# Swapping the halves of queries and keys: transfers within the on-chip memory in place of products with signed permutations

## The reference, cut to what matters

```python
def apply_rope(x, cos, sin):
    half = x.shape[-1] // 2
    x1, x2 = x[..., :half], x[..., half:]
    return jnp.concatenate([x1 * cos - x2 * sin, x1 * sin + x2 * cos], axis=-1)

qa = axial_rope(rms_norm(qa, q_norm_a), cos_r, sin_r, cos_c, sin_c)   # A: 8 heads of 64, rotated in two groups of 32
ka = axial_rope(rms_norm(ka, k_norm_a), cos_r, sin_r, cos_c, sin_c)   # A: 2 key heads
q_rope = apply_rope(q_rope, cos_t, sin_t)                             # B: 8 heads, 32 features of each
k_rope = apply_rope(kr, cos_t, sin_t)                                 # B: one key part of 32 features
```

## Time and profile before

| | us |
|---|---|
| median of three runs | 2465.02 (2460.68 to 2466.03) |
| span of the profiled execution | 2457.9 |
| PE busy | 2368.7 (96%) |
| DVE busy | 1412.9 (57%) |
| ACT busy | 1138.7 (46%) |
| POOL busy | 894.2 (36%) |

### The profile page before, as it was taken

How to read it: one execution, slowest core, us unless ns; L and a number is a source line. 1 busy time by engine, 2 the same in 40 slices (tenths; PEclk the granted TensorE clock), 3 DMA queues, 4 the chain that set the end, 5 groups by cost and what they waited for, 6 DMA issues and landing times.

```text
span 2457.9 us, 31373 instructions
## 1 busy us (share of the span) xinstructions
PE 2368.7 (96%) x12074; PEld 1954.5 (80%) x12074; DVE 1412.9 (57%) x1963; ACT 1138.7 (46%) x1778; POOL 894.2 (36%) x665
## 2 busy tenths in 40 slices
PE   5999999989999999999999999999999999999998
PEld 5778788868888888876678877788878888888887
DVE  6255499958885330139963753332576666666665
ACT  5322388868884221249952474231333333333334
POOL 1111234236652112335521222112255555555651
PEclk8999999999999999999999999999999999999999
DMA  7244300000003131100031311013111111111121
GB/s 301 75 129 145 94 6 1 1 19 1 1 1 112 59 108 43 52 1 1 10 112 38 121 44 43 18 35 120 43 52 52 52 52 52 52 52 52 52 60 69
DMA packets 152487, 143.21 MB, mean 58 GB/s; under 512 B 10358, under 2 KB 140692, under 8 KB 150420
## 3 DMA queue, kind: packets, MB, share of 16 engines
q1 hardware_dynamic: 152340, 141.22, 18.0%
HBM read 124.43 MB, written 16.78 MB: 57 GB/s over the span
## 4 chain that ended last, share of the span: by engine, by line
PE 81%; ACT 8%; issue 5%; DVE 4%; POOL 1%; DMA 1%; SPq 0%; ACTq 0%; DVEq 0%; POOLq 0%
PE ps L260 38%; PE ps L2608 14%; PE ps L2625 9%; PE ps L1103 4%; PE ps L1126 3%; PE ps L1113 3%; ACT C_PR L1773 1%; ACT B_PR L1186 1%; ACT B_PTH L1180 1%; PE ps L2584 1%; PE ps L1662 1%; ACT C_PTH L1781 1%; PE ps L2052 1%; PE ps L2064 1%; PE ps L1641 1%
## 5 line engine op out<-in xcount | busy, mean ns | idle before, releaser
L249 POOL TENSOR_TENSOR WL<-WR,WH 128x1024 fp32r<-128x1024 f32 (+1 forms) x89 | 207.5, 2332 | 827.3 <-ACT WH L244 827.2
L260 PE MATMUL ps<-HH,WH 128*128 128x512 f32 (+1 forms) x1136 | 362.3, 400 | 0.0
L260 PE MATMUL ps<-HL,WH 128*128 128x512 f32 (+1 forms) x1136 | 353.4, 392 | 0.0
L260 PE MATMUL ps<-HH,WL 128*128 128x512 f32 (+1 forms) x1136 | 352.7, 392 | 0.0
L260 PEld LDWEIGHTS ps<-HL,WH 128*128 128x128 f32 (+1 forms) x1136 | 213.9, 188 | 47.3
L260 PEld LDWEIGHTS ps<-HH,WL 128*128 128x128 f32 (+1 forms) x1136 | 213.9, 188 | 47.1
L260 PEld LDWEIGHTS ps<-HH,WH 128*128 128x128 f32 (+1 forms) x1136 | 210.0, 189 | 51.8 <-issue 10.1
L2838 DVE TENSOR_TENSOR XF<-ps,XF 128x1024 f32<-128x1024 f32 x168 | 201.5, 1220 | 32.4 <-PE ps L2625 25.8
L2608 PE MATMUL ps<-HC,WSH 128*128 128x512 f32 x640 | 197.0, 389 | 0.0
L1139 DVE TENSOR_REDUCE NM<-ps 128x1 f32<-128x1024 f32 x128 | 156.0, 1220 | 35.0 <-PE ps L1103 34.1
L2525 POOL TENSOR_TENSOR WSL<-WSR,WSH 128x512 fp32r<-128x512 f32 x100 | 131.0, 1310 | 107.6 <-ACT WSH L2519 107.6
(11 more groups left out here) (433 smaller groups left out, 5227.2 us busy)
## 6 DMA issues: line engine op xcount, KB each, us to landing
WS<-in_w_ffn_in SPq DMA_DIRECT2D x44, 512.0 KB, 5.0
MKW<-in_ada_w SPq DMA_DIRECT2D x32, 512.0 KB, 4.1
spill<-X SPq DMA_DIRECT2D x3, 4096.0 KB, 13.6
OW<-in_w_ffn_out SPq DMA_DIRECT2D x22, 512.0 KB, 3.4
WR<-in_w_in SPq DMA_DIRECT2D x20, 512.0 KB, 3.6
WR<-in_odd_w_in SPq DMA_DIRECT2D x19, 512.0 KB, 3.7
WR<-in_even_w_in SPq DMA_DIRECT2D x17, 512.0 KB, 4.8
AWK<-in_ada_w SPq DMA_DIRECT2D x8, 1024.0 KB, 9.4
```

What stands on the lines that cost most here:

```text
L249: pool.tensor_tensor(low[:, :, :], raw[:, :, :], high[:, :, :].bitcast(F32), ALU.subtract).then_inc(*w_low.up(t))
L260: last = pe.matmul(ps[0:w.m, 2 * s + h, :], wt[:, k, :], x[:, k, halves(h)], start=(k == 0 and n == 0), stop=(k == w.kt - 1 and n == 2))
```

## The change

The permutation matrices `SWAPA` and `SWAPB` and all products with them go. In their place SP copies, for each rotation, every block of 16 partitions of `RG0` (for B: `BG`) into its neighbour's place in `RT2` (`BT2`), one transfer of 16 rows of 4 KB for each block: eight for a tile of 128 features, two for KR. The signs move into the sine tables. DVE waits for the last of the transfers (`swap_landed`) and reads the swapped values from `RT2` and not from PSUM. In SP's program the eight transfers stand at tile j = 6+r behind the load of weights and ahead of the blocks of `ada_w`, and wait for ACT's copy of the tile and for `rope_added(r-1)`, since `RT2` has one buffer. PE's waits that guarded banks 6 and 7 go or change. `BT2` has two buffers now. On the host side only constants change.

```diff
-                     swapA=swap(HD // 2), swapB=swap(B_ROPE), ... sinA=np.sin(ang_a), ... sinB=np.sin(ang_b)
+    ... sinA=np.sin(ang_a) * turned_sign(HD // 2), ... sinB=np.sin(ang_b) * turned_sign(B_ROPE)
...
+    def sp_swap(r, src, dst, parts, width=16):
+        for b in range(parts // width):
+            sp.dma_start(dst[rows(b, width), :], src[rows(b ^ 1, width), :]).then_inc(*rope_swapped[r % 2].landed(r, b))
+    def swap_landed(r, parts, width=16):
+        return rope_swapped[r % 2].at(r, parts // width - 1)
...
             if j == 5:
+                sp.wait_ge(*ev_act.at(EVEN_KR))
+                sp_swap(KR, RG0[:, (KR + 1) % 2, :], RT2, B_ROPE)
                 sp.wait_ge(*lat_low.at(2))
+            elif 6 <= j < 11:
+                r = j - 6
+                sp.wait_ge(*rope_copied.at(r))
+                sp.wait_ge(*rope_added.at(r - 1))
+                sp_swap(r, RG0[:, (r + 1) % 2, :], RT2, P)
             for n in MOD_ROWS.get(j, ()):
                 sp_mod_rows(n)
...
-        dve.tensor_tensor(t2, pair(6, rows_), sin[rows_, :], ALU.mult).then_inc(*rope_parts.up(r, 0))
+        dve.tensor_tensor(t2, t2, sin[rows_, :], ALU.mult).then_inc(*rope_parts.up(r, 0))
...
+                pe.wait_ge(*ev_act.at(EVEN_QK[r]))
                 pe_rope_norm(r).then_inc(*rope_mm.up(r))
...
-                pe.wait_ge(*rope_parts.at(2 if m == 0 else 4, 0))
+                if m == 0:
+                    pe.wait_ge(*lat_scaled.at(2))
                 pe_mod_sums(m)
...
-                pe_rope_swap(EVEN_KR, KR, SWAPB, slice(0, B_ROPE)).then_inc(*rope_mm.up(KR))
...
-                    pe_rope_swap(EVEN_QK[r], r, SWAPA)
...
+                dve.wait_ge(*swap_landed(r, P))
                 dve_rope_add(r, QKA[:, QK_ORDER[r], :], COSA, SINA)
...
-        for t in B_PROJ[2:]:
+        for i, t in enumerate(B_PROJ[2:], 2):
             sp_weights(t)
+            if 5 <= i < 7:
+                r = i - 5
+                sp.wait_ge(*ev_act.at(B_PROJ[2 + r]))
+                sp_swap(B_ROT + r, BG[:, (r + 1) % 2, :], BT2[:, r, :], P)
...
-                pe_rope_swap(B_PROJ[2 + r], r, SWAPB, G=BG).then_inc(*rope_mm.up(f"B{r}"))
```

More of the change, by code:

```diff
@@ L48, in shape_constants, with turned_sign @@
     blk64 = np.kron(np.eye(2), np.ones((HD, HD))).astype(f)
[L50 to L59, removed]
+    def turned_sign(width):
+        return np.where(np.arange(P) % width < width // 2, -1.0, 1.0)[:, None]
     def angles(pos, dim):
@@ L75, in shape_constants @@
     inside = np.tile((tok % CHUNK != 0).astype(f)[None, :], (P, 1))
-    parts = dict(ident=ident, blk64=blk64, swapA=swap(HD // 2), swapB=swap(B_ROPE),
-                 slopes=slopes, away=away, cosA=np.cos(ang_a), sinA=np.sin(ang_a),
-                 cosB=np.cos(ang_b), sinB=np.sin(ang_b), inside=inside)
+    parts = dict(ident=ident, blk64=blk64, slopes=slopes, away=away, cosA=np.cos(ang_a), sinA=np.sin(ang_a) * turned_sign(HD // 2),
+                 cosB=np.cos(ang_b), sinB=np.sin(ang_b) * turned_sign(B_ROPE), inside=inside)
     at, where = 0, {}
@@ L698, in build @@
     SINA, RT2, RWD = place("SINA", 99.5, [P, SEQ]), place("RT2", 103.5, [P, SEQ]), place("RWD", 107.5, [P, SEQ])
-    SWAPA, BLK, SWAPB = place("SWAPA", 43, [P, P]), place("BLK", 43.5, [P, P]), place("SWAPB", 79, [P, P])
+    BLK = place("BLK", 43.5, [P, P])
     COSB, SINB = place("COSB", 111.5, [P, SEQ]), place("SINB", 115.5, [P, SEQ])
@@ L732, in sp_even_proj @@
                 sp.wait_ge(*n_low.at(0, DT - 1))
-                for i, (dst, n) in enumerate(((COSA, "cosA"), (SINA, "sinA"), (SWAPA, "swapA"), (BLK, "blk64"), (COSB, "cosB"),
-                                              (SINB, "sinB"), (SWAPB, "swapB"))):
+                for i, (dst, n) in enumerate(((COSA, "cosA"), (SINA, "sinA"), (BLK, "blk64"), (COSB, "cosB"), (SINB, "sinB"))):
                     sp.dma_start(dst[:, :], const(n)).then_inc(*tables_in.landed(i))
             if j == 5:
+                sp.wait_ge(*ev_act.at(EVEN_KR))
+                sp_swap(KR, RG0[:, (KR + 1) % 2, :], RT2, B_ROPE)
                 sp.wait_ge(*lat_low.at(2))
+            elif 6 <= j < 11:
[3 more added lines that the diff above has]
+                sp_swap(r, RG0[:, (r + 1) % 2, :], RT2, P)
             for n in MOD_ROWS.get(j, ()):
@@ L749, in act_rope_copy @@
         act.activation(RSQ[rows_, r % 2, :], pair(2 * (t % 2), rows_), ACT.Square).then_inc(*ev_act.up(t))
[L751 to L756, removed]
     def pe_rope_norm(r):
@@ L828, in pe_even_proj @@
             elif j == 4:
-                pe.wait_ge(*tables_in.at(6))
+                pe.wait_ge(*tables_in.at(4))
                 pe_latent_turn(0)
@@ L832, in pe_even_proj @@
             elif j == 5:
[L833 to L834 removed]
+                pe.wait_ge(*lat_scaled.at(1))
                 pe.wait_ge(*ev_act.at(EVEN_V))
@@ L838, in pe_even_proj @@
                 last.then_inc(*va_turned.up())
[L839 to L846, removed]
-                    pe_rope_swap(EVEN_QK[r], r, SWAPA)
+            elif 7 <= j < 12:
+                pe_rope_turn(j - 7)
     def act_latent(c):
@@ L945, in dve_even_proj @@
         dve_latents()
-        dve.wait_ge(*rope_mm.at(KR))
+        dve.wait_ge(*tables_in.at(4))
+        dve.wait_ge(*swap_landed(KR, B_ROPE))
         dve_rope_add(KR, KRR[0:B_ROPE, :], COSB, SINB, slice(0, B_ROPE))
@@ L1287, in pool_attention_a @@
         pool_dense(A, beside)
-    BG, BT2 = place("BG", 63, [P, 2, SEQ]), place("BT2", 196, [P, SEQ])
+    BG, BT2 = place("BG", 63, [P, 2, SEQ]), place("BT2", 192, [P, 2, SEQ])
     B_SCALE = (B_NOPE + B_ROPE) ** -0.5
@@ L1364, in dve_b_proj @@
             g, dst = BG[:, (r + 1) % 2, :], QR[:, r, :]
[L1365 to L1368, removed]
+            dve.wait_ge(*swap_landed(B_ROT + r, P))
+            dve.tensor_tensor(BT2[:, r, :], BT2[:, r, :], SINB[:, :], ALU.mult).then_inc(*rope_parts.up(f"B{r}", 0))
             dve.tensor_tensor(g, g, COSB[:, :], ALU.mult).then_inc(*rope_parts.up(f"B{r}", 1))
             dve.wait_ge(*rope_parts.at(f"B{r}", 1))
-            dve.tensor_tensor(dst, BT2[:, :], g, ALU.add).then_inc(*rope_added.up(f"B{r}"))
+            dve.tensor_tensor(dst, BT2[:, r, :], g, ALU.add).then_inc(*rope_added.up(f"B{r}"))
         for piece in (3, 4):
```

9 lines of the change are left out of this document (2 added, 7 removed).

## The result

| | before | after |
|---|---|---|
| median of four runs, us | 2465.53 (2460.68 to 2468.97) | 2488.36 (2484.45 to 2493.20) |
| ratio, with its 95% interval | 1 | 1.0101 (1.0083 to 1.0120) |
| span of the profiled execution, us | 2457.9 | 2484.9 |

The changed kernel is 1.0% slower, +27.0 us between the two profiled spans. I had forecast +11.7 us and a range that ended at 2487, 1.4 us under the median. The ratio in the table is not the quotient of the two medians, which is 1.0093: the loss is 22.8 us by the medians, 24.9 by the ratio and 27.0 between the two traces. The direction and the mechanism are those of the forecast, the size is about twice what I had summed.

What follows compares the result with a forecast made beforehand. PE was taken to bound the kernel (81% of the chain); A's longer turns and slow starts cost 14.0 us, B's projection gives back 2.3, net +11.7: 2476.7 us. Own range 2469.6 to 2482.3; 8 in 10, 2467 to 2487.

Steps and rivals of the forecast that it cites:

- The mechanism: A's turns: `ada_w` blocks wait behind rotation and swap issues, so PE waits for DVE; turns 20.6 or 17.3 us.
- What goes: PE's swap products: 10.4 us go for KR and five of A, 2.3 us in B's projection.
- The rest of the program: Later tiles and attention A move as one by 14.0 us; B's projection gives back 2.3.
- eight issues: SP, each turn of A: eight swap issues at 0.37 us, 3.0 us; bounds 2.5 and 3.8.
- DVE beside POOL: DVE's copy and additions in A's turns: the prediction had no term for this, 0 us.
- landings of blocks: `ada_w` blocks in A's turns: first lands 3.7 us after issue (bounds 3.4 and 4.3), third 3.4.
- slow sums: PE's square sums after waits of 6.9, 3.6 and 6.9 us: 1.7 us longer each, 5.1 in all.
- start of rotation 0: Square sums of rotation 0 begin at 143.9 us, from 147.44 less 1.83 and 1.72.
- Of the rivals, 1: Swap transfers themselves delay `ada_w` blocks: each turn grows 2.0 us, four by 8.0, to 2484.7; chance 0.17.
- estimate of 4.8 us: Time for the eight swap transfers if 16 neighbouring partitions reach a quarter of the ports, from 435 GB/s.
- estimate of 10 us: One issue in place of eight takes some 2.6 us out of every turn, 10 of the 14.0.
- Rival 3: Hold on SP costs nothing, all removed products are gain, 10.4 + 2.3 = 12.7 us: 2452.3; chance 0.10.

Runs made afterwards that it cites:

- e8: Changed kernel with series of transfers added behind its end; eight 16-row issues within SBUF took 5.0 us, from DRAM 3.6.
- e9: Changed kernel with DVE operations added behind its end, alone and then beside POOL's difference; three additions took 3.67 us alone, 9.90 beside.
- e3: Changed kernel with one 128-row transfer in place of eight per rotation of A, halves not swapped; 2467.53 us against 2460.58 before, ratio 1.0023.
- e1: Changed kernel with the `ada_w` blocks of tiles 6 to 10 issued ahead of the eight swap transfers; 2451.45 us against 2460.58 before, ratio 0.9956.
- e6: Kernel before with only KR and B's two rotations swapped by transfers, A's still by products; 2458.56 us against 2462.15, ratio 0.9989.
- e5: Changed kernel with 42, 32, 14, 42 small PE products ahead of square sums of rotations 1 to 4; 2491.36 us against 2462.15 before, ratio 1.0113.

## Why the prediction fell short

Right, by its own steps:

- **The mechanism.** DVE adds, SP issues, the block comes, DVE adds blocks and scales, PE starts: the chain after is that list, link by link. The waits of PE are largest in turns 0 and 3 and smallest in turn 2, as worked out, and the square sums ran at the low clock after the three that I named. That the clock would hold after the fourth was wrong: it fell behind the sums of rotation 3 (0.55 from 216 to 218 us), which cost only 0.3 us because DVE held that turn.
- **What goes.** Square sums of rotation 0 start at 143.02, I had 143.9 (0.7 of the difference PE had ahead of the first product that went, 128.53 for 129.19). B gave back 1.9 us for 2.3. The sine product from SBUF takes 1.21 us, as before from PSUM. The swap is never what DVE waits for in A's loop.
- **The rest of the program** follows tile 12 by the same 30.4 to 30.5 us until B. Behind B the difference shrinks from 28.5 to 27.0; I did not follow that 1.5 us.

Wrong was the size. Tile 12's sums had to move by 14.0 us and moved by 30.4, 16.4 too little. By the steps of the turns (those of the prediction against the times in the chain above):

| step | foreseen | measured | over 4 turns |
|---|---|---|---|
| eight issues, each turn | 3.0 us | 5.05 | +8.2 |
| SP late to begin, turn 1 | 0 | 0.5 | +0.5 |
| DVE beside POOL: copy (turn 0), pair (turn 1), addition (turn 3) | 0 | 1.2 + 2.0 + 1.5 | +4.7 |
| landings of blocks, turns 0, 1 and 3 | 3.7, 3.4 | 3.7 to 3.9, 3.6 to 3.8 | +1.0 |
| slow sums, three turns, and the tile behind rotation 4 | 5.1 | 8.0 | +2.9 |
| start of rotation 0 | 143.9 | 143.02 | -0.9 |

The sum is 16.4. **The step that failed is the price of "eight issues"**: I took 3.0 us from the load of the convolution weights from DRAM, the nearest row, and called 3.8, by a 128-row load from DRAM, the upper bound, though neither was a transfer within SBUF. The price is 5.0 (the changed kernel and e8), half of the miss, and it was knowable only as unknown: with no row of that form the upper end had to lie far above the nearest one. The second is a term that my sum put at nothing without a reason, DVE beside POOL: when a chain moves in time it comes to stand beside other work. DVE's copy and additions came to stand beside POOL's difference, 4.7 us (overlap in the traces, the effect shown by e9). The last is the clock behind rotation 4: I counted the sums (1.7) but not the products after them, 10.36 us for 36 where the tile takes 8.33 at full clock.

Of the rivals, 1 gave 2484.7, nearest to the result, by luck: it let each block land 2.0 us later, and the landings grew by 0.0 to 0.4 us, while e3 takes most of the loss away with the same bytes. The estimate of 4.8 us that I drew from the port rule of the Trainium skill, "SBUF — State Buffer", "Door 1: The DMA port swizzle", is not tested by this: the eight issues took 5.0 us, and transfers that drain in 4.8 could be done by then. The advice of "DMA: Bandwidth & Descriptors" in the Trainium skill, "Rules for kernel authors", to use one transfer over all partitions came with an estimate of 10 us; e3 shows 19. Rival 3, the other side, needed the blocks in time, and e1 is that kernel: 12.7 us of gain foreseen, and measured 0.44% of 2461, 10.8 us, by its ratio, 8.0 between the traces. Of the 4.7 us that are missing between the traces, 2.0 are PE's waits in the loop and about 2 the low clock behind them. Its condition was named rightly, and it takes two statements in another order.

## What to carry to other kernels

A transfer put into an in-order queue costs everything behind it its wait and its issues, so it belongs behind the prefetches that do not need it; here the same change is worth +1.0% or -0.4% by that alone (e1, the best version measured). Where the trace has no row for a form of transfer, rows of other forms give its issue no upper bound: measure a series of it first, or keep the range open upward. And when a chain is shifted, look at what other engines do at its new place, POOL beside DVE above all. A gain on one engine goes only as far as the next thing that it waits for: in e6 PE was 2.0 us earlier at tile 12 and 0.35 us at attention A.

## What the runs showed of the hardware

- Transfers within SBUF over 4, 16 or 64 partitions, issued one behind another, hold SP for 0.59 to 0.63 us each, with rows of 512 B as of 4 KB; from DRAM over 16 partitions 0.45; one within SBUF over all 128 partitions, alone, 0.48 (e8).
- DVE's additions, copies and products with all operands in SBUF took 3.3 us for 1.2, 2.82 for 0.68 and up to 3.36 for 1.21 beside POOL's difference (e9), and POOL's own went from 2.34 to a median of 3.05.
- Behind a wait of 2.91 us the granted clock was 0.50 (e5, 278 to 283 us) and the sums took 3.58 us; behind one of 1.06 us (after, rotation 3) the sums took 1.96, near the 1.68 of full clock, and the clock fell only behind them, to 0.55 from 216 to 218 us.
